# First layer's r by seven products instead of eight, behind q and k

## The reference, cut to what matters

```python
q, k, v, r, g_low = split(x @ w_in)          # q,k: 512 wide; v,r: 1024 wide; g_low: 16 wide
log_a = log_sigmoid(g_low @ w_gate_up + b_gate) / 16
q_dec, k_inv, k_end = q*exp(cum), k*exp(-cum), k*exp(total-cum)   # cum: running sum of log_a
a = where(causal, q_dec @ k_inv.T, 0);  o = a @ v + q_dec @ state
state = state * decay + k_end.T @ v
o = normalise(o) * norm_g                    # per head of 256
y = (silu(r) * o) @ w_out
```

## Time and profile before

| what | value |
|---|---|
| median of three runs | 1132.1 us |
| the profiled execution's own time | 1132.14 us |
| its span | 1130.4 us |
| TensorE's granted clock over the span | 0.999 of full |
| PE busy | 1120.2 us, 99% |
| DVE, ACT, POOL busy | 784.6, 569.8, 325.6 us |
| share of the last chain that is PE | 96% |

### The profile page before, as it was taken

One profiled execution on the slowest core, in us unless ns is written; L12 is line 12 of the kernel. 1 busy time (PEld: TensorE's weight loads), 2 busy tenths in 40 slices (PEclk: granted clock), 3 DMA queues, 4 the chain that ended last, 5 costly groups with the idle time before them and its releaser, 6 DMA issues.

```text
span 1130.4 us, 18412 instructions
## 1 busy us (share of the span) xinstructions
PE 1120.2 (99%) x6828; PEld 994.7 (88%) x6828; DVE 784.6 (69%) x1263; ACT 569.8 (50%) x926; POOL 325.6 (29%) x215
## 2 busy tenths in 40 slices
PE   9999999999999999999999999999999999999997
PEld 7888888989999999888887787778989999998886
DVE  5070163798888885998604676766878888868987
ACT  4345144244555556555515565772445555556553
POOL 1538525142222112000445343551412222230001
PEclk9999999999999999999999999999999999999999
DMA  6433314076897764654332212132159879827551
GB/s 227 167 150 112 112 38 149 13 271 164 273 279 211 245 182 175 234 197 170 108 112 75 95 47 94 48 150 75 38 191 279 237 248 280 214 74 298 189 193 75
DMA packets 34459, 183.35 MB, mean 162 GB/s; under 512 B 3152, under 2 KB 7376, under 8 KB 20704
## 3 DMA queue, kind: packets, MB, share of 16 engines
q1 hardware_dynamic: 19472, 122.27, 30.1%
q0 software_dynamic: 8448, 46.14, 15.8%
q10 hardware_dynamic: 6480, 14.17, 3.5%
HBM read 180.46 MB, written 51.38 MB: 205 GB/s over the span
## 4 chain that ended last, share of the span: by engine, by line
PE 96%; DVE 1%; issue 1%; DMA 1%; ACT 0%; POOL 0%; SPq 0%; DVEq 0%; POOLq 0%; ACTq 0%
PE bank L2057 29%; PE bank L2059 29%; PE bank L2058 29%; PE bank L2509 2%; PE bank L2493 2%; PE bank L2140 1%; PE bank L2088 1%; PE bank L2530 1%; PE bank L2529 1%; DMA s_raw<-stream 1%; PE bank L2338 1%; DVE s_w_lo L1330 1%; PE bank L2331 0%; PE bank L2346 0%; PE bank L2324 0%
## 5 line engine op out<-in xcount | busy, mean ns | idle before, releaser
L2057 PE MATMUL bank<-s_t_hi,s_w_hi 128*128 128x256 f32 (+1 forms) x832 | 264.4, 318 | 0.0
L2058 PE MATMUL bank<-s_t_lo,s_w_hi 128*128 128x256 f32 (+1 forms) x832 | 262.8, 316 | 0.0
L2059 PE MATMUL bank<-s_t_hi,s_w_lo 128*128 128x256 f32 (+1 forms) x832 | 262.8, 316 | 0.0
L1179 POOL TENSOR_TENSOR s_w_lo<-s_raw,s_w_hi 128x1024 fp32r<-128x1024 f32 x64 | 160.1, 2512 | 180.3 <-ACT s_w_hi L638 180.3
L638 ACT ACTIVATE s_w_hi<-s_raw 128x1024 fp32r<-128x1024 f32 x107 | 111.3, 1057 | 114.6 <-PE bank L2059 90.5
L2059 PEld LDWEIGHTS bank<-s_t_hi,s_w_lo 128*128 128x128 f32 x832 | 158.6, 191 | 10.2
L2057 PEld LDWEIGHTS bank<-s_t_hi,s_w_hi 128*128 128x128 f32 x832 | 158.7, 191 | 9.7 <-issue 0.2
L2058 PEld LDWEIGHTS bank<-s_t_lo,s_w_hi 128*128 128x128 f32 x832 | 158.7, 191 | 9.4
L1216 POOL TENSOR_TENSOR s_w_lo<-s_raw,s_w_hi 128x512 fp32r<-128x512 f32 x36 | 67.2, 1866 | 274.3 <-ACT s_w_hi L768 274.3
L2057 PE MATMUL bank<-s_t_hi,s_w_s_hi 128*128 128x256 f32 x432 | 122.4, 283 | 0.0
L2059 PE MATMUL bank<-s_t_hi,s_w_s_lo 128*128 128x256 f32 x432 | 122.2, 283 | 0.0
(11 more groups left out here) (246 smaller groups left out, 2489.0 us busy)
## 6 DMA issues: line engine op xcount, KB each, us to landing
s_raw<-stream SPq DMA_DIRECT2D x75, 1024.0 KB, 4.8
sums<-down POOLq DMA_DIRECT2D x12, 2816.0 KB, 20.9
s_more_raw<-sums SPq DMA_DIRECT2D x12, 1024.0 KB, 4.9
sums<-sums POOLq DMA_DIRECT2D x4, 2816.0 KB, 12.9
s_raw<-down SPq DMA_DIRECT2D x8, 1024.0 KB, 4.9
s_ln_gb<-ln_gb ACTq DMA_DIRECT2D x4, 1024.0 KB, 7.0
s_more_raw<-down SPq DMA_DIRECT2D x4, 1024.0 KB, 7.5
s_raw<-sums SPq DMA_DIRECT2D x4, 1024.0 KB, 4.9
```

The source lines that it names most:

```text
L1179: nc.gpsimd.tensor_tensor(lo, raw_pair(SLOTS[place // 2])[:, n % 2, cols], hi.bitcast(F32), ALU.subtract).then_inc(lo_done, new)
L2057: nc.tensor.matmul(out, l_hi, r_hi, start=start, stop=False, skip_group_check=skip)
L2058: nc.tensor.matmul(out, l_hi, r_lo, start=False, stop=False, skip_group_check=skip)
L2059: return nc.tensor.matmul(out, l_lo, r_hi, start=False, stop=stop, skip_group_check=skip)
```

## The change

1. **Order of the slabs.** v, then q and k (8), then r, then the output projection. The gate's four matmuls (`gate_up`) now stand behind q's first slab. The pair of the last head is no longer swapped.
2. **r in seven products.** r's weight matrix is cut in 2 x 2 blocks of 512 x 512, the tokens in two halves and the inputs in two halves. Instead of eight products of halves, seven are made of sums of blocks. A product is 4 input blocks x 2 token tiles x 3 terms = 24 matmuls of 512 columns. Each takes four 128 x 512 blocks of weights, two slabs, so r takes 14 slabs instead of 8, and a slab feeds 12 matmuls instead of 24.
3. **Sums of weights.** POOL issues eight transfers of 1 MB (`r_block_sum`, every other one accumulating) that make four sums in DRAM (`r_sums`), each behind the one before it (`pool.wait_ge(r_blocks, 16 * step)`), two slabs' low parts apart. SP loads r's slabs from `r_down` and `r_sums`.
4. **Sums of tokens.** DVE makes three sums (128 x 1024) and a fourth in two pieces (128 x 512) from `x_t` while v is multiplied, ACT makes high parts and DVE low parts (`r_op_highs`, `r_op_low`). They lie in the room of `h` and `ln_gb`, whose loads from DRAM move from behind v to behind product 5 of r.
5. **Merging.** Products add up in four pairs of banks x, y, z, w. ACT copies x and y to `g_rg` at four points (`r_copy`), DVE adds or subtracts the other banks (`r_add`, eight of 128 x 512), then ACT applies silu in place (`r_silu`), POOL multiplies by `norm_g` (`scale_r`).
6. **q and k.** The first two heads' banks are copied by ACT to `qk_raw` (`copy_qk`), since the decay factors are not ready; the last two heads are multiplied straight from PSUM, their banks being used by r only in its second and third product.
7. **Low parts.** r's slabs from its third on, and the output projection's first four slabs (`GLA_OUT` to `GLA_OUT + 3`), are split by DVE instead of POOL. Two of those four stand between the steps of the recurrence.
8. **Before r's last product** PE makes the transposes and the scores of tile 0.

The core of the diff:

```diff
-GLA_R = GLA_V + KD
-GLA_QK = GLA_R + KD
-GLA_OUT = GLA_QK + 2 * GLA_HEADS
+GLA_QK = GLA_V + KD
+GLA_R = GLA_QK + 2 * GLA_HEADS
+GLA_OUT = GLA_R + 2 * 7
...
+        R_BANKS = {"x": (0, 1), "y": (6, 7), "z": (4, 5), "w": (2, 3)}
+        R_QUARTERS = ((0, 0), (1, 0), (0, 1), (1, 1), (2, 1), (3, 1), (2, 0), (3, 0))
...
             for n in range(GLA_V, GLA_R):
-                split_lo(n + RING)
+                if n + RING < GLA_R + 2:
+                    split_lo(n + RING)
+                if n % 2 == 1:
+                    r_block_sum(n // 2)
...
+            r_low(4, 7)
+            dve.wait_ge(slab_done, GLA_R + 4)
+            dve.wait_ge(r_copied, 2)
+            r_add(0, None, "z", ALU.add)
+            r_add(1, None, "z", ALU.add)
+            r_low(7, 10)
+            dve.wait_ge(r_op_hi, 4)
+            r_op_low(0, g_rg[:, 2:4, 0:HALF].rearrange("p t (k c) -> p t k c", k=2))
+            r_low(10, 14)
+            dve.wait_ge(slab_done, GLA_R + 10)
+            dve.wait_ge(r_copied, 6)
+            r_add(2, "y", None, ALU.subtract)
+            r_add(3, "y", None, ALU.subtract)
+            split_low(GLA_OUT)
+            dve.wait_ge(r_copied, 8)
+            r_add(4, None, "x", ALU.subtract)
+            r_add(5, None, "x", ALU.subtract)
...
+            mask_scores(0)
+            split_low(GLA_OUT + 1)
+            dve.wait_ge(slab_done, GLA_R + 14)
+            r_add(6, None, "w", ALU.add)
+            r_add(7, None, "w", ALU.add)
...
-            mask_scores(0)
+            split_low(GLA_OUT + 2)
             update_state(0)
             mask_scores(1)
+            split_low(GLA_OUT + 3)
             stats_o(0)
...
-            token_major(1, GLA_R, lambda half, t: 4 - 4 * half + t, r_free, beside=gate_up)
...
+            for p in range(PRODUCTS):
+                if 1 <= p <= 2:
+                    pe.wait_ge(qk_scaled, 3 * (GLA_HEADS - 2 + p))
+                if 2 <= p <= 5:
+                    pe.wait_ge(r_op_lo, p - 1)
+                if 3 <= p <= 5:
+                    pe.wait_ge(r_copied, 2 * (p - 2))
+                if p == PRODUCTS - 1:
+                    pe.wait_ge(consts, 7)
+                    pe.wait_ge(r_merged, 2)
+                    turn_ke(0)
+                    gla_scores(0)
+                op_hi_, op_lo_ = r_operand(p)
+                for j in range(KD // 2):
+                    n = GLA_R + 2 * p + j // 2
+                    if j % 2 == 0:
+                        pe.wait_ge(lo_done, place_of(n) + 1)
+                    for i in range(2):
+                        toks = slice(i * P, (i + 1) * P)
+                        last = three(bank[R_BANKS[INTO[p]][i]][:, :], op_hi_[:, j, toks], op_lo_[:, j, toks],
+                                     *w_parts(n, slice(j % 2 * HALF, (j % 2 + 1) * HALF)),
+                                     INTO[p] not in INTO[:p] and j == 0, j == KD // 2 - 1, True)
+                    if j % 2:
+                        last.then_inc(slab_done, 1)
...
                 pe.wait_ge(sc_masked, t + 1)
+                if t == 0:
+                    pe.wait_ge(r_merged, 2 * TILES)
```

More of the change, by code:

```diff
@@ L180, in build_program @@
         t_lo = sb("t_lo", [P, KD, SEQ], F32R)
+        h_at = place[0]
         h = sb("h", [P, TILES, D_MODEL])
@@ L653, in load_gb, with token_major @@
                 act.dma_start(ln_gb[:, :, :], a["ln_gb"][n].partition_broadcast(P)).then_inc(gb_full, 16)
-            def token_major(which, n0, bank_of, copy_out):
+            def token_major(which, n0, bank_of, copy_out, between=None):
                 for half in range(2):
+                    if half == 1 and between is not None:
+                        between()
                     for k in range(KD // 2):
@@ L903, in _ @@
                 nc.scalar.activation(low_rows[group * LOW:group * LOW + GLA_RANK, :], g_part[0:GLA_RANK, :],
[L904 removed]
+                                     ACT.Copy).then_inc(rows_hi, 1)
             for hd in range(GLA_HEADS):
@@ L935, in _, with r_split, r_done, r_copy @@
-            for n in range(GLA_QK, GLA_OUT - 1):
-                split_hi(n + RING)
+            def r_split(first, end):
+                for slab in range(first, end):
+                    split_hi(GLA_R + slab)
+            def r_done(p):
+                act.wait_ge(slab_done, GLA_R + 2 * p + 2)
+            def r_copy(b, quarter):
+                t, half = R_QUARTERS[quarter]
+                nc.scalar.activation(g_rg[:, t, half * HALF:(half + 1) * HALF], bank[R_BANKS[b][t % 2]][:, :],
+                                     ACT.Copy).then_inc(r_copied, 1)
@@ new lines, in r_silu @@
+            def r_silu(quarter):
+                t, half = R_QUARTERS[quarter]
+                act.wait_ge(r_merged, quarter + 1)
+                nc.scalar.activation(g_rg[:, t, half * HALF:(half + 1) * HALF], g_rg[:, t, half * HALF:(half + 1) * HALF],
+                                     ACT.Silu).then_inc(tok_out[1], 1)
+            r_split(1, 5)
+            r_done(0)
+            act.wait_ge(qk_scaled, 6)
+            r_copy("x", 0)
+            r_copy("x", 1)
+            r_split(5, 8)
@@ new lines, in _ @@
+            r_silu(0)
+            r_silu(1)
+            r_split(8, 9)
+            r_done(2)
+            act.wait_ge(r_op_sum, 4)
+            nc.scalar.activation(r_ops[0]["hi"][:, :, :], g_rg[:, 2:4, 0:HALF].rearrange("p t (k c) -> p t k c", k=2),
+                                 ACT.Copy).then_inc(r_op_hi, 1)
+            r_copy("y", 4)
+            r_copy("y", 5)
+            r_split(9, 11)
+            r_done(3)
+            r_copy("x", 2)
+            r_copy("x", 3)
+            r_split(11, 14)
@@ L938, in ke_tile_out @@
+            for n in range(GLA_OUT, GLA_OUT + 2):
+                split_hi(n)
+            r_silu(2)
+            r_silu(3)
+            r_done(5)
+            act.dma_start(h[:, :, :], a["x"].rearrange("(t p) d -> p t d", p=P)).then_inc(h_full, 16)
+            load_gb(0)
+            act.wait_ge(r_op_lo, 4)
+            r_copy("x", 6)
+            r_copy("x", 7)
             def ke_tile_out(t):
@@ L1264, in _ @@
                 nc.gpsimd.tensor_tensor(rstd_o[:, t, :], var_eps_o[:, t, :], minus_half[:, :], ALU.pow).then_inc(o_rstd, 1)
+            for quarter in range(8):
+                scale_r(quarter)
+            for t in range(TILES):
+                root_o(t)
+            pool.wait_ge(lo_done, GLA_OUT + TAIL)
             for n in range(FFN_IN[0], FFN_IN[0] + TAIL):
@@ L1823, in _, with r_low @@
+            def r_low(first, end):
+                for slab in range(first, end):
+                    split_low(GLA_R + slab)
             for hd in range(GLA_HEADS):
-                for i, scale_part in enumerate((scale_k, scale_q) if hd == GLA_HEADS - 1 else (scale_q, scale_k)):
-                    dve.wait_ge(slab_done, GLA_QK + 2 * hd + i + 1)
-                    scale_part(hd)
+                if hd >= 2:
+                    if hd == 2:
+                        dve.wait_ge(lo_done, GLA_R + 2)
+                    r_low(hd, hd + 1)
+                for i, scale_part in enumerate((scale_q, scale_k)):
+                    if hd < 2:
+                        dve.wait_ge(qk_copied, 2 * hd + i + 1)
+                    else:
+                        dve.wait_ge(slab_done, GLA_QK + 2 * hd + i + 1)
+                    scale_part(hd)
@@ new lines, in r_add @@
+            def r_add(quarter, first, second, op):
+                t, half = R_QUARTERS[quarter]
+                out = g_rg[:, t, half * HALF:(half + 1) * HALF]
+                first, second = (out if b is None else bank[R_BANKS[b][t % 2]][:, :] for b in (first, second))
+                nc.vector.tensor_tensor(out, first, second, op).then_inc(r_merged, 1)
+            r_low(4, 7)
+            dve.wait_ge(slab_done, GLA_R + 4)
+            dve.wait_ge(r_copied, 2)
+            r_add(0, None, "z", ALU.add)
```

218 lines of the change are left out of this document (127 added, 91 removed).

## The result

The changed kernel took **1126.5 us** (median of 5 executions, 1126.1 to 1127.1) against 1132.15 us before: ratio 0.995, 95% interval [0.9935, 0.9965], or 5.6 us less (4.0 to 7.4). Forecast were 1127.0 us, 5.1 less than before. The profiled execution took 1126.1 us, its span is 1124.3.

A forecast was written before the change was run, and what follows sets the result against it. PE, busy 99% of the span, was taken as the bound: its instructions laid end to end. Terms 1 and 2, -5.44 + 0.3 = -5.1 us, gave 1127.0 us, range 1126.3 to 1130.0.

The forecast's parts named there:

- Term 1: r's matmuls on PE: 24 fewer at 0.2265 us each, worth 5.44 us.
- the floor of the prediction: Least possible time, PE's shorter list with nothing lost: 1132.1 - 5.44 = 1126.7 us.
- Term 2: Work that must hide behind PE's shorter list, tight only in the recurrence: 0 to 0.7 us lost, taken as 0.3.
- Sums of tokens: On DVE during v: 8.6 us, 16 us even with POOL's work between, within 29.0 us idle; costs nothing.
- The chain of sums: POOL's eight serial 1 MB transfers for r's weights: at 7.6 us each no cost, threshold 11.7 us each.
- d: Time of one 1 MB sum of weights, bounded by 4.7 and 20.9 us, taken as 7.6.
- the prediction's signs of being wrong: PE waiting over 1 us for a state, low part or raw slab, or one sum taking over 11 us.
- the third rival: Chain of sums long, with POOL standing in it: at d = 13.5, 14.4 us added, 1141 us; chance 6%.
- Feed of r's slabs: Loading and splitting r's slabs: 8.3 us per round against PE's 10.9; no cost up to 7.4 us landing.
- The second rival: r's slabs come late: pairs land in 9 us, 4.8 us lost in r, 1131.8 us, no difference; chance 7%.
- The first rival: DVE falls behind in the recurrence, low parts waiting out POOL's multiplications: PE loses about 2.8 us, 1129.5 us; chance 14%.

## Why the prediction was right, step by step

**Term 1, 24 x 0.2265 = 5.44 us**: right. The result is -5.6, doing a product twice costs 5.2, and read from the gate's matmuls to the end the profiles give 5.3 to 5.5. The 0.2 us by which the median lies beyond the floor of the prediction is within the spread of single executions.

**Term 2, the recurrence, 0 to 0.7, taken 0.3**: it came out as 0. The timetable held: updates(0) at 137.28 against 137.8, and all of that is where the whole execution began its work sooner (DVE's step behind the gate stands at 54.04 where it stood at 54.65; the gate's own matmuls, line 2440, start at 58.66 and at 58.97 in two executions of the changed kernel). The stall did not come since the low part in front of state 0 began first: at 138.59, 0.2 us ahead of POOL's last pair of multiplications at 138.81. So it took its 1.21 us, and POOL's pair was the one held, 3.37 us instead of 2.56. The prediction priced only the other case, DVE held by POOL. The lead is the program's and not luck of one start, though it is small: POOL's pair needs ACT's silu of the merges that stand directly in front of this low part on DVE, and in the second profile of the changed kernel and in the one with transposes and scores behind product 6 it is 0.2 us again. The silu's row:

```profile
138.10 1.24 ACT L967 ACTIVATE s_g_rg<-s_g_rg 128x512 f32<-128x512 f32 x2 [1.54 <-DVE s_g_rg L1950]
```

So the state had 0.9 us to spare, where 0.7 was forecast without collision. The low parts at 135.50 and 141.67 began while POOL was multiplying and did wait (1.97 and 1.59 us). The last mask, forecast for 154.8 to 155.8 against 155.3, came at 154.27 against 154.65: 0.4 to spare, the same 0.4 as before the change. The 11.04 us from the first statistics to that mask repeated as 11.05.

**Sums of tokens, "even with 3 of POOL's 2.5 us in between 16 us"**: mis-sized. They took 22.4 us. All eight of DVE's instructions there stretched, the 128 x 1024 sums to 3.3 us and the low parts to 3.0, where 1.2 is usual, and the two half sums to 1.8, where 0.7 was forecast, since POOL's low parts ran beside them. Of the 29.0 idle us 6.7 were left, so it cost nothing, as forecast, but with half of the margin that I had. The rule that I had cited (SBUF — State Buffer, "Who interferes with whom" of the Trainium skill) gives this, the trace agrees with it at 3.3 us; I applied it to three instructions where it held for eight.

**The chain of sums, d = 7.6 with a threshold at 11.7**: the threshold was right, the timetable below it was not. The last sum landed at 112.0, where "all landed by 110" was forecast and 31 + 8 x 7.6 gives 92. Of the 81.6 us from the first issue (30.4) to that landing 68.8 are transfers, 8.6 us each on average instead of 7.6. The other 12.8 are steps that were not issued when the one before had landed. 9.0 of them stand in front of the fifth, which was issued at 74.57 though the fourth had landed at 65.5: two of POOL's low parts come first in its order, and they had waited for ACT's high parts. One of the prediction's signs of being wrong did show: the fourth sum took 11.7 us, over the 11 named there. It cost nothing, because the sign was set on a single sum while the threshold is on the mean of eight, and here even on the landing at 125. One transfer more is free, three cost 9.5 us: the third rival was a real mechanism, nearly two transfers away.

**Feed of r's slabs, up to 7.4 us of landing**: the loads took 4.8 and 5.0 us, PE waited for none. The second rival fell.

**The first rival, DVE behind in the recurrence, 2.8 us**: did not happen, but it is the nearest. Two more low parts cost 4 to 5 us, leaving transposes and scores behind product 6 costs 2.6. Its reason counted each low part as held by POOL; one of the three was not.

**What no step had**: a price of the clock. In each rival a wait of PE was priced at its length. Measured, a wait of 4.1 us cost about 1.7 more, and one of 5.6 us (three transfers more in the chain of sums) was followed by 0.50 of the clock as well, with PE, DVE and ACT busy and no transfer under way (one of its windows, columns as above):

```profile
138.00:139.00 1.00, 1.00 (x3) 0.81 (x4) 1.00 (x2) 1.00 (x2) 0.00 (x0) 0.50 0.00 0
```

In the profile with two more low parts a wait of 3.6 us left it at 1.00, but nine of that run's eleven executions, and five of the eleven with the low parts between POOL's multiplications (waits of 2.2 and 1.0 us in its profile), ran at a mean clock of 0.995 to 0.997 and took about 1 to 3 us longer than the rest. So the price is not the same in every execution, and a profile that shows none does not rule it out. Rival three, with a wait of 14.4 us, was then probably a little too cheap; no run had a wait that long.

## What to carry to other kernels

When TensorE is busy for 99% of the span, price a change by the instructions it removes from TensorE's list, and spend the rest of the time on a timetable of who is asked for what and when; here the slack was 0.9 and 0.4 us, and three of the arrangements that looked like details (late use of two banks, low parts off POOL, scores one product early) are worth 6.4, 2.1 to 4.0 and 2.6 us each. When you move work from GpSimd to VectorE, count as long every VectorE instruction with both inputs in SBUF that begins while GpSimd multiplies or subtracts, the shortest too; where VectorE begins first, GpSimd's is the long one. So ask which of the two begins first, and what fixes that order. A wait of TensorE is not always priced by its length: look at the granted clock of the stretch behind it, and at the mean clock of the executions that were not profiled. A serial chain of transfers that an engine issues between other work is as long as the transfers and that engine's turns together.
